# A scratch in DRAM that holds each bias row 128 times, and no stage that flips the tiles

## The reference, cut to what matters

```python
x = _layer_norm(DN_ALPHA * x + 0.5 * _swiglu(x, ffn1_w1[l], ffn1_w2[l]), ln1_g[l], ln1_b[l])
mix = _token_mix(x, w_in[l], ..., rel_bias, ...)
...
dist = W + i[:, None] - j[None]
band = (dist >= 0) & (dist < W)
bias = rel_b.reshape(G, HPG, REL_BUCKETS)[:, :, _t5_bucket(dist)]
logits = jnp.where(mask, logits + bias[:, :, None], -jnp.inf)
```

## Time and profile before

| | us |
|---|---|
| median of 3 runs | 2818.55 |
| lowest and highest run | 2815.96, 2820.69 |
| span of the profiled execution, first to last instruction | 2815.3 |
| PE busy in it | 2644.5 (94%) |
| DVE busy | 1284.8 (46%) |
| ACT busy | 1059.5 (38%) |

### The profile page before, as it was taken

How to read it: one execution, slowest core, us unless ns; L and a number is a source line. 1 busy time by engine, 2 the same in 40 slices (tenths; PEclk the granted TensorE clock), 3 DMA queues, 4 the chain that set the end, 5 groups by cost and what they waited for, 6 DMA issues and landing times.

```text
span 2815.3 us, 40283 instructions
## 1 busy us (share of the span) xinstructions
PE 2644.5 (94%) x16574; PEld 1948.3 (69%) x16574; DVE 1284.8 (46%) x2355; ACT 1059.5 (38%) x1748; POOL 69.0 (2%) x28
## 2 busy tenths in 40 slices
PE   8999999999999999999989899999888999998996
PEld 8988988899898988889888654433336864433433
DVE  5565554755756565475677651111116653111112
ACT  4444563444444465344457631111114442111110
POOL 0001000100100100010010000000000000000000
PEclk9999999999999999999999999999999999999999
DMA  9645633565463853446354289999996229999997
GB/s 308 220 118 157 215 97 115 195 198 193 155 206 107 228 164 105 162 158 204 109 180 130 87 339 416 420 421 421 421 418 210 91 96 421 421 420 421 421 421 290
DMA packets 315366, 695.37 MB, mean 247 GB/s; under 512 B 58224, under 2 KB 243440, under 8 KB 266032
## 3 DMA queue, kind: packets, MB, share of 16 engines
q1 hardware_dynamic: 312000, 682.09, 66.1%
q10 hardware_dynamic: 3184, 10.69, 1.2%
HBM read 691.65 MB, written 1.08 MB: 246 GB/s over the span
## 4 chain that ended last, share of the span: by engine, by line
PE 64%; DMA 19%; DVE 10%; ACT 5%; issue 2%; SPq 1%; ACTq 0%; DVEq 0%
PE ps L295 26%; DMA ring<-in_moe_w_gate 8%; PE ps L2619 7%; PE ps L827 7%; DMA slots_over_xT<-in_moe_w_gate 6%; DMA moe_slots<-in_moe_w_gate 5%; PE ps L1605 3%; PE ps L2669 3%; PE ps L1645 3%; DVE weight_parts L226 3%; PE ps L334 2%; PE ps L306 2%; ACT weight_parts L218 1%; PE ps L2555 1%; SPq L2521 1%
## 5 line engine op out<-in xcount | busy, mean ns | idle before, releaser
L295 PE MATMUL ps<-xT_upper,weight_parts 128*128 128x256 f32 (+1 forms) x4656 | 843.4, 285 | 17.8 <-DVE arena L2241 7.5
L226 DVE TENSOR_TENSOR weight_parts<-ring,weight_parts 128x1024 fp32r<-128x1024 f32 x479 | 611.2, 1279 | 489.8 <-ACT weight_parts L218 489.2
L295 PEld LDWEIGHTS ps<-xT_upper,weight_parts 128*128 128x128 f32 (+1 forms) x4656 | 717.2, 189 | 41.5 <-DVE weight_parts L226 13.7
L218 ACT ACTIVATE weight_parts<-ring 128x1024 fp32r<-128x1024 f32 x479 | 504.0, 1055 | 533.4 <-PE ps L295 321.0
L295 PE MATMUL ps<-xT_lower,weight_parts 128*128 128x256 f32 (+1 forms) x2328 | 649.8, 283 | 1.9 <-DVE xT_lower L988 1.5
L295 PEld LDWEIGHTS ps<-xT_lower,weight_parts 128*128 128x128 f32 (+1 forms) x2328 | 437.3, 189 | 3.6 <-DVE xT_lower L988 2.8
L2619 PE MATMUL ps<-ring,bias_tiles 128*64 128x512 f32 x1024 | 243.1, 595 | 27.9 <-DMA ring<-in_moe_w_gate 16.0
L2914 DVE TENSOR_TENSOR arena<-ps,arena 128x512 f32<-128x512 f32 x32 | 22.1, 692 | 475.2 <-ACT arena L2782 475.2
L827 PE MATMUL ps<-weight_parts,hidden_upper 128*128 128x512 f32 x704 | 218.3, 391 | 4.4 <-DVE hidden_lower L880 4.4
L2619 PEld LDWEIGHTS ps<-ring,bias_tiles 128*64 128x64 f32 x1024 | 78.9, 137 | 182.9 <-issue 126.2
L2782 ACT ACTIVATE arena<-ps 128x512 f32<-128x512 f32 x32 | 19.2, 599 | 494.9 <-PE ps L2619 494.9
(11 more groups left out here) (335 smaller groups left out, 3191.0 us busy)
## 6 DMA issues: line engine op xcount, KB each, us to landing
ring<-in_ffn_w SPq DMA_DIRECT2D x132, 1024.0 KB, 5.2
ring<-in_moe_w_up SPq DMA_DIRECT2D x64, 1024.0 KB, 26.8
ring<-in_moe_w_gate SPq DMA_DIRECT2D x64, 1024.0 KB, 26.3
ring<-in_moe_w_down SPq DMA_DIRECT2D x64, 1024.0 KB, 26.7
moe_slots<-in_moe_w_up SPq DMA_DIRECT2D x48, 1024.0 KB, 26.6
moe_slots<-in_moe_w_down SPq DMA_DIRECT2D x40, 1024.0 KB, 26.6
slots_over_xT<-in_moe_w_gate SPq DMA_DIRECT2D x32, 1024.0 KB, 27.5
moe_slots<-in_moe_w_gate SPq DMA_DIRECT2D x32, 1024.0 KB, 26.2
```

Of the source, the lines that this page charges most:

```text
L218: act.activation(self.part(n, 0), cut(self.stream.slot(pos)), ACT.Copy).then_inc(self.upper_done, 1)
L226: dve.tensor_tensor(self.part(n, 1), cut(self.stream.slot(pos)), self.part(n, 0).bitcast(F32), ALU.subtract).then_inc(self.split, 1)
L295: m = pe.matmul(out[0:rows, :], w[of_w][:, k, :], c.xTp[of_x][:, k, :], start=(at == 0), stop=(at == len(steps) - 1))
```

## The change

The scratch grows from 16 rows of 512 numbers to 16 x 128 rows of 384: each head's row is written 128 times, one behind the other. Read with a step of 383 instead of 384 from partition to partition, and starting at place 127, each partition's 256 numbers begin one place earlier than those of the partition before it. So the tiles arrive in the right order, and the constants already carry the factor 1/SCALE. The stage that flips the tiles, its matrix and the load of it are gone.

The store of the rows moves out of the setup stage, to ACT's queue behind chunk 4 of the first feed-forward stage. It reads 16 partitions, writes 2048 rows of 1536 B (3.1 MB) and has a source with a step of 0. The load of the tiles (2 MB, as before) moves in SP's queue from ahead of position 8 to between positions 17 and 18; it still waits for the store to land.

```diff
-        self.scratch = nc.dram_tensor("bias_scratch", [16, 512], F32, kind="Internal").ap()
+        self.scratch = nc.dram_tensor("bias_scratch", [16, P * SKEW], F32, kind="Internal").ap()
...
-        sp.dma_start(flip_matrix(c), a["c_flip"]).then_inc(c.const_landed.sem, 16)
...
-        act.wait_ge(c.setup_dve.sem, 2)
-        act.dma_start(c.scratch, brow[0:16, :]).then_inc(c.stored.sem, 16)
...
+def store_bias_rows(c, act):
+    rows = bias_rows(c)[0:16, 0:SKEW]
+    act.wait_ge(c.setup_dve.sem, 2)
+    act.dma_start(c.scratch.rearrange("h (p n) -> h p n", p=P),
+                  bass.AP(rows.tensor, rows.offset, [rows.ap[0], [0, P], [1, SKEW]])).then_inc(c.stored.sem, 16)
     c.stored.issued += 16
...
     sp.wait_ge(c.stored.sem, 16)
-    sp.dma_start(E_v, bass.AP(c.scratch.tensor, 0, [[1, P], [512, 16], [1, S]])).then_inc(c.bias_landed.sem, 16)
+    sp.dma_start(E_v, bass.AP(c.scratch.tensor, P - 1, [[SKEW - 1, P], [P * SKEW, 16], [1, S]])).then_inc(c.bias_landed.sem, 16)
...
-def flip_bias_stage(c):
...
+BIAS_AT = 4
...
-            if load_first:
-                load_first(c, sp)
+            if bias:
+                s.issue(sp, BIAS_AT * 3 + AHEAD)
+                load_bias_tiles(c, sp)
             s.issue(sp, plan.end + AHEAD)
...
+                if n == BIAS_AT and bias:
+                    store_bias_rows(c, act)
...
         def _(dve):
+            if bias:
+                dve.wait_ge(c.setup_dve.sem, 2)
...
-            if l == 0:
-                flip_bias_stage(c)
```

More of the change, by code:

```diff
@@ L51 @@
 CLOCK_ROWS, CLOCK_PARTS, CLOCK_ROUTER = (512, 512), 1024, (1024, 2560, 512, 512)
-CONSTANTS = 7 + 4 * DEPTH
+CONSTANTS = 6 + 4 * DEPTH
+SKEW = 384
 NORMS = 10
@@ L632, in setup_stage @@
     bmask = c.take(512)
-    brow = c.E[:, 0:512]
+    brow = bias_rows(c)
     s = c.stream
@@ L709, in setup_stage @@
     c.small.issued += 32
-    c.stored.issued += 16
     c.next_stage()
@@ L717, in bias_tile, with bias_rows @@
     return c.E[:, h * S:(h + 1) * S]
-def flip_matrix(c):
-    return c.E[:, 17 * S + 2048:17 * S + 2048 + P]
+def bias_rows(c):
+    return c.E[:, 0:512]
+def store_bias_rows(c, act):
[3 more added lines that the diff above has]
+                  bass.AP(rows.tensor, rows.offset, [rows.ap[0], [0, P], [1, SKEW]])).then_inc(c.stored.sem, 16)
+    c.stored.issued += 16
 def load_bias_tiles(c, sp):
@@ L778, in __init__, with ffn_stage @@
         self.end = len(s.loads)
-def ffn_stage(c, plan, load_norm, load_first=None):
+BIAS_AT = 4
+def ffn_stage(c, plan, load_norm, bias=False):
     ps, s, block = c.ps, c.stream, c.block
@@ L941, in _ @@
         ch = c.dve_chain
+        dve.wait_ge(c.const_landed.sem, 16 * CONSTANTS)
         def side(t, h):
@@ L1021, in _ @@
     def _(act):
+        act.wait_ge(c.const_landed.sem, 16 * CONSTANTS)
         def deviation(t):
@@ L1308, in close_compressed @@
             mm.then_inc(K.cmp_ps.sem, K.cmp_ps.one())
-        if c.aux_act.issued:
-            pe.wait_ge(c.aux_act.sem, c.aux_act.issued)
-            pe.wait_ge(c.aux_dve.sem, c.aux_dve.issued)
+        pe.wait_ge(c.const_landed.sem, 16 * CONSTANTS)
         for g in range(TILES):
@@ L1798, in cmp_probs @@
                 ins.then_inc(K.cmp_probs.sem, K.cmp_probs.one())
-            for sig in (P_.log_act, P_.kept_act, P_.kept_dve, P_.cmp_hidden, c.rows, c.aux_act):
+            for sig in (P_.log_act, P_.kept_act, P_.kept_dve, P_.cmp_hidden, c.rows):
                 dve.wait_ge(sig.sem, sig.issued)
+            dve.wait_ge(c.bias_landed.sem, 16)
+            dve.wait_ge(c.const_landed.sem, 16 * CONSTANTS)
             dve.memset(b["cmp_p"].rearrange("p g s i n -> p (g s i n)"), 0.0)
@@ L3349, in build @@
         for l, (ffn1, mix, ffn2) in enumerate(plans):
-            done, lead = ffn_stage(c, ffn1, norm_loader(c, a["ln1_g"][l], a["ln1_b"][l]), load_bias_tiles if l == 0 else None)
+            done, lead = ffn_stage(c, ffn1, norm_loader(c, a["ln1_g"][l], a["ln1_b"][l]), bias=(l == 0))
             norm_stage(c, 0.5, done, lead=lead)
-            if l == 0:
-                flip_bias_stage(c)
             done, lead = token_mix(c, mix, l, norm_loader(c, a["ln2_g"][l], a["ln2_b"][l]))
@@ L3383, in constants @@
     k["c_ident"] = np.eye(P, dtype=f)
-    k["c_flip"] = np.eye(P, dtype=f)[::-1].copy()
     dist = 255 - np.arange(512)
@@ L3387, in constants @@
     onehot[t5_bucket(dist), np.arange(512)] = 1
-    k["c_onehot"] = onehot * (dist >= 0)
+    k["c_onehot"] = onehot * (dist >= 0) * f(1 / SCALE)
     bmask = np.zeros((16, 512), f)
-    bmask[:, dist < 0] = NEG
-    bmask[8:, dist >= 128] = NEG
+    bmask[:, dist < 0] = NEG / SCALE
+    bmask[8:, dist >= 128] = NEG / SCALE
     k["c_bmask"] = bmask
```

## The result

| | before | after |
|---|---|---|
| median of 4 runs, us | 2819.1 | 2854.2 |
| lowest and highest run | 2815.96, 2820.69 | 2852.89, 2854.67 |
| span of the profiled execution | 2815.3 | 2852.9 |
| mean granted clock in it | 0.989 | 0.979 |

The change makes the kernel slower by 35.1 us: ratio 1.0128, 95% interval 1.0116 to 1.0140. The prediction was 2838.5 us with a range that ended at 2848. The direction came out as argued, the size did not: 15.7 us are missing from the sum. Part of the 3.25 us that the forecast put between span and median was chance: the median of the changed kernel stands 1.3 us above its span. In span, 2835.5 was forecast and 2852.9 measured, so 17.4 us are missing.

What follows compares the result with a forecast made beforehand. PE was taken to bound both changed places, 64% of the last chain. From a span of 2815.3, -11.5 + 29.8 + 1.9 gave 2835.5 us, with 3.25 to the median 2838.7, stated as 2838.5; range 2812 to 2848.

Steps and rivals of the forecast that it cites:

- Term 1: Layer 0, zeros to compression products: without flips it becomes a copy of layer 1, 50.31 to 38.81 us, -11.5 us.
- My check in the profile: Sign to look for: no flips, and the compression products 38.8 us behind the last products of zeros.
- Term 2: First feed-forward stage: PE waits +29.8 us in front of chunk 6 for a weight load queued behind store and tile load.
- S: Time from the store's issue to its landing, estimated at 31.2 us; PE's wait is S - 1.4.
- The pair behind the store: Tile load and next weight load in SP's queue after the store lands, taken as 12.8 us from the earlier trace.
- The middle in ratio between 211 and 53 GB/s: Store rate from 16 partitions, taken as 106 GB/s between the 64-partition rate and one falling in proportion to partitions.
- the port rule: Trainium skill: transfers limited by ports reached, 27 GB/s each; partitions 0 to 15 reach 4, 104 GB/s measured, store 30.4 us.
- Term 3: After PE's wait in front of chunk 6 the granted clock falls, as after 2.92 us of idling: +1.9 us.
- What else changes costs nothing: Flip matrix's load, store's old place and added waits, for constants and tiles landed long before, were taken as 0 us.
- (a): Rival: store not held back much, landing in 8.9 to 16.4 us, total 2816.5 to 2824 us; chance 0.17.
- (b): Rival: store rate falls on to about 53 GB/s, landing in 60.9 us, total 2868.5 us; chance 0.13.
- (c): Rival: tile and weight loads behind the store take 10.6 instead of 12.8 us, total 2812.3 us; chance 0.08.

Runs made afterwards that it cites:

- the kernel with both cures: Changed kernel, store still from 16 partitions, tile load behind position 29 in SP's queue, norm-stage waits for constants moved to the first feed-forward stage: 2813.27 us, ratio 0.9979.
- the kernel with 16 products: The kernel with both cures plus 16 small products of zeros on PE in the setup stage: 2808.25 us, ratio 0.9968 to the kernel before.

## Why the prediction was off

- **Term 1, the flips gone, -11.5 us: right.** Between the first and the second mark of the changed kernel 11.0 us are won (33.8 to 22.8), and 11.5 in the kernel with both cures (+0.25 to -11.2), where no exposed table load stands between. My check in the profile was off by a detail: the compression products come 277.68 - 240.39 = 37.3 us behind the zeros (the last zeros start at 240.39), not 38.8. Both layers have 37.3 now, and so has layer 1 in the second trace of the kernel before. The 38.8 held one fall of the clock, in layer 1 of the first trace and not of the second (columns as in the earlier trace rows: the third from the end is the granted clock):

```profile
935.00:940.00 5.00, 4.44 (x24) 4.44 (x25) 3.11 (x4) 3.79 (x6) 0.00 (x0) 0.66 1.21 225
```

```profile
937.00:942.00 5.00, 4.57 (x38) 4.57 (x39) 3.10 (x5) 4.96 (x9) 0.00 (x0) 1.00 1.25 227
```

  So to this point the change wins 13.0 us, and that the sum's 11.5 fits the later mark is in part luck. It ends as 11 to 11.5 at the next mark, since the clock falls elsewhere in the stage as well, by chance of the execution; in the kernel with 16 products, with one fall less, the stage is 13.0 us shorter than before (296.4 against 309.4).
- **Term 2, PE's wait of 29.8 us: right**, measured 30.0. S was estimated as 31.2 and is 32.5. The pair behind the store took 11.8 us instead of 12.8, so two errors of about 1 us cancelled. The middle in ratio between 211 and 53 GB/s happened to hit 104. That was luck as far as the trace of before goes; the runs with 32, 64 and 128 partitions agree with the port rule, which I could have given more weight than a middle.
- **Term 3, the clock behind the stall, 1.9 us: right in kind**, 2.5 measured. With 8.3 us of idling it cost about the same (14.11 us for those products).
- **The step that failed is the sentence "What else changes costs nothing"**, with its reason that "the added waits are for constants and tiles that landed long before". I asked only what a wait waits for, not what it stands ahead of. The wait was satisfied at once, and it still cost 7.6 to 9.1 us over the nine norm stages, because it pushed an older wait onto the table load. The order of the changed kernel's instructions, with their waits, shows this before any run.
- **The same sentence left out a second cost**: the removed instructions move every later one of PE. Dilated attention is 3.9 us longer after (191.1 against 187.2), 2.2 of it the new wait; the rest goes with lower clock around it (9.7 us lost instead of 6.4).

The ledger for the two first traces: 30.4 (chunk 6 late) + 2.5 (clock behind it) - 11.5 (flips) + 7.6 to 9.1 (table loads) + 3.9 (dilated attention) = 32.9 to 34.4, of 37.6. The other 3.2 to 4.7 us are of the size by which two traces of one kernel differ (3.5 and 3.6 us). The largest piece is the second token mixing, 5.2 us longer with 8.5 instead of 1.7 us lost to the clock; the second traces of both kernels show that it swings by 3 us by itself. Why the clock falls there stays open. Of the 35.1 us between the medians 0.7 to 2.2 are left.

The rivals: (a) a store at over 200 GB/s is what 32 or 64 partitions give, not 16; (b) is out; (c), a quicker pair behind the store, was 1 us right, and no more.

## What to carry to other kernels

A wait that never waits can cost time: read which instruction each wait ends up on, above all where a table load stands ahead of an ACTIVATE. Here a long transfer from few partitions did no harm once no early weight load queued behind its consumer: placing the dependent load later won some 30 us, and a store from eight times the partitions after that nothing. When instructions are removed, compare the "issue" waits at the start of later, untouched stages too.

## What the runs showed of the hardware

- A DMA store from SBUF ran at 104, 215, 215 and 372 GB/s from 16, 32, 64 and 128 partitions, with the DMA engines 0.9 to 1.03 busy once it ran steadily. Their busy share doesn't tell whether they move data or wait for it.
- A table load of 1.28 us is hidden or exposed by which of two neighbouring instructions carries a wait: 0.8 us for each where the clock holds, and in all +9.1 us by adding the wait and 7.6 to 9.0 less by moving it.
- Without the flips, PE waits 1.9 to 3.2 us at a place in its own instruction stream, released by nothing that the profile shows, and one product more at the program's start moves that place by two matmuls, 2 ms later.
